# RWKV pairs pipelined: the next pair of heads' projections among the present pair's block steps, its last norm beside the next pair's levels

## The reference, cut to what matters

```python
r, k, v = jnp.einsum('ibtd,ide->ibte', xm[:3], w_rkv)
w = -jax.nn.softplus(-(w0 + jnp.tanh(xw @ w1) @ w2)) - 0.5
decay = jnp.exp(-jnp.exp(w))
a = jax.nn.sigmoid(a0 + (xa @ a1) @ a2)
g = jax.nn.sigmoid(xg @ g1) @ g2
kk = heads(k * k_k);  kk = kk / max(norm(kk), 1e-12)
kf = heads(k * (1.0 + (a - 1.0) * k_a))
def step(S, inp):                       # over the tokens, per head
    sa = einsum('bhij,bhj->bhi', S, -kk_t)
    S = S * w_t + sa (x) (kk_t * a_t) + v_t (x) k_t
    return S, einsum('bhij,bhj->bhi', S, r_t)
yn = (y - mean) * rsqrt(var + GN_EPS) * ln_w + ln_b     # per head
out = ((yn + sum(rf * kf * r_k) * vf) * g) @ w_o
```

## Time and profile before

| | us |
|---|---|
| median of 3 runs | 4031.53 |
| lowest and highest | 4029.28, 4032.35 |
| the profiled execution | 4034.49 |
| its span, first to last instruction | 4032.7 |
| busy TensorE, VectorE, ScalarE, GpSimd | 3435.5, 2789.6, 1501.1, 1424.4 |

### The profile page before, as it was taken

One profiled execution on the slowest core, in us unless ns is written; L12 is line 12 of the kernel. 1 busy time (PEld: TensorE's weight loads), 2 busy tenths in 40 slices (PEclk: granted clock), 3 DMA queues, 4 the chain that ended last, 5 costly groups with the idle time before them and its releaser, 6 DMA issues.

```text
span 4032.7 us, 46671 instructions
## 1 busy us (share of the span) xinstructions
PE 3435.5 (85%) x15384; PEld 1899.4 (47%) x15384; DVE 2789.6 (69%) x6464; ACT 1501.1 (37%) x4296; POOL 1424.4 (35%) x1272
## 2 busy tenths in 40 slices
PE   5999988869988888988989888989899888778876
PEld 3777777645443333444445443545454333333322
DVE  5555555545766666888886777898857777777775
ACT  1333333313433333534444434433435343333333
POOL 0011100013544444434443444333335444444442
PEclk8888999889999999999999999999999999999999
DMA  2110000049999999999999999999989999999996
GB/s 78 29 31 24 25 24 24 17 169 399 427 427 427 427 427 426 413 391 424 409 405 399 415 426 425 399 347 346 358 338 421 427 425 427 426 427 426 427 424 291
DMA packets 229603, 1310.45 MB, mean 325 GB/s; under 512 B 58736, under 2 KB 61936, under 8 KB 81648
## 3 DMA queue, kind: packets, MB, share of 16 engines
q0 software_dynamic: 165888, 1208.03, 72.3%
q1 hardware_dynamic: 63472, 99.43, 7.0%
HBM read 1301.52 MB, written 5.86 MB: 324 GB/s over the span
## 4 chain that ended last, share of the span: by engine, by line
DMA 30%; PE 25%; DVE 18%; ACT 3%; issue 2%; DVEq 1%; ACTq 1%; POOL 0%; POOLq 0%
DMA arena<-in_uv,arena 30%; PE psum L1157 15%; DVE arena L1585 8%; PE psum L1121 4%; PE psum L1209 3%; DVE arena L1675 3%; ACT wbuf L1375 1%; DVE arena L1649 1%; DVE arena L1513 1%; PE psum L1168 1%; ACT arena L1370 1%; PE psum L1229 1%; DVE arena L1510 0%; DVE arena L1652 0%; DVE arena L1517 0%
## 5 line engine op out<-in xcount | busy, mean ns | idle before, releaser
L1157 PE MATMUL psum<-arena,wbuf 128*128 128x512 f32 (+1 forms) x4608 | 2096.5, 629 | 442.9 <-ACT wbuf L1375 441.7
L1101 POOL DMA_INDIRECT arena<-in_uv,arena x1152 | 1349.8, 1172 | 1825.1 <-PE psum L1157 1677.9
L1585 DVE SCALAR_TENSOR_TENSOR arena<-arena 128x1024 f32<-128x1024 f32 x1152 | 1393.4, 1222 | 530.8 <-DMA arena<-in_uv,arena 514.8
L1157 PEld LDWEIGHTS psum<-arena,wbuf 128*128 128x128 f32 (+1 forms) x4608 | 811.0, 191 | 1533.2 <-issue 785.8
L1366 ACT ACTIVATE arena<-arena 128x2 f32<-128x2 f32 x576 | 116.9, 203 | 1666.9 <-DVE arena L1585 1666.1
L1375 ACT ACTIVATE wbuf<-cst,arena 128x128 f32<-128x128 f32 (+1 forms) x1152 | 392.7, 388 | 41.3 <-issue 1.7
L1121 PE MATMUL psum<-arena,wbuf 128*128 128x256 f32 (+1 forms) x1024 | 290.8, 430 | 8.7 <-DVE arena L1596 5.8
L1370 ACT ACTIVATE arena<-arena 128x1 f32<-128x1 f32 x1152 | 276.9, 287 | 40.7 <-issue 1.0
L1121 PEld LDWEIGHTS psum<-arena,wbuf 128*128 128x128 f32 x1024 | 203.3, 201 | 127.9 <-issue 88.8
L1675 DVE SCALAR_TENSOR_TENSOR arena<-arena,par 128x256 f32<-128x256 f32 x368 | 177.6, 483 | 47.8 <-ACT arena L1431 32.1
L842 POOL COPY arena<-arena 128x256 f32<-128x256 f32 x8 | 3.2, 397 | 584.0 <-DVE arena L735 584.0
(11 more groups left out here) (265 smaller groups left out, 3213.1 us busy)
## 6 DMA issues: line engine op xcount, KB each, us to landing
wbuf<-in_w_q SPq DMA_DIRECT2D x64, 576.0 KB, 9.2
arena<-in_w_pw SPq DMA_DIRECT2D x48, 512.0 KB, 10.4
arena<-in_uv,arena POOLq DMA_INDIRECT x1152, 19.0
wbuf<-in_w_rkv SPq DMA_DIRECT2D x24, 512.0 KB, 3.6
wbuf<-in_w_o SPq DMA_DIRECT2D x8, 512.0 KB, 3.5
arena<-in_w_o SPq DMA_DIRECT2D x8, 512.0 KB, 7.7
x<-in_x SPq DMA_DIRECT2D x1, 2304.0 KB, 8.1
arena<-in_state SPq DMA_DIRECT2D x16, 128.0 KB, 3.0
```

The costliest lines, as they stand in the source:

```text
L1101: pool.indirect_dma_start(ring[:, g % RING, :], None, I["uv"][p // 2], bass.IndirectOffsetOnAxis(ap=idx[:, s % 4, j:j + 1], axis=0)).then_ ...
L1157: last = pe.matmul(out, diag[:, g % DIAGS, 0:P if u < NB else NS], ring[:, g % RING, D + e * 512:D + (e + 1) * 512], start=head == 0 and j ...
L1585: stt(out=row, in0=row, scalar=1.0, in1=tok[p % 2][:, UNITS[p % 2].index(u), :], op0=ALU.mult, op1=ALU.mult, accum_out=dots[:, g % COLS:g ...
```

## The change

The passes are written out as a pipeline over pairs.

- **Projections.** A generator `front(n)` yields after each product of pair n: 2 steps for `w` with `a` (now per half of the columns, banks 2 and 3), 48 products for `k`, `r` and `v`, and 2 sums of the norm. In pass i, TensorE's block steps draw from `front(i + 1)` at fifteen places, 48 steps in all (1 ahead of R0, 1 ahead of U0, 2 ahead of Y0, 6 ahead of R1, then 3, 3, 5, 3, 3, 4, 3, 3, 3 up to Y3, 4 behind it and 4 behind `s_Y`), and the last 4 behind the mean. `front(0)` stands ahead of the first pass. All of it uses banks 2 and 3; R, U and S now share bank 0, and Y stands in bank 1. ScalarE's evictions are made per half and stand among the copies of R and U; VectorE's front stands among the state updates.
- **Last norm.** `last_norm(i - 1)` is a generator too: reciprocal in four parts, scale, bias and gain, bonus, gate. VectorE takes two steps of it after each of the first five levels of pass i.
- **Samples' state.** The two operations L821 and L823 move from before the norm to behind pass i + 1's masks, ahead of its first level.
- **Transposes.** `tok_v`, `tok_b` and `tok_k` move from ahead of the grams into levels 1, 2 and 3.
- **Buffers.** `g_s`, `bon`, `esc` and `ln` become double; `y_s`, `yc`, `ysq`, `sd`, the samples' scratch, `sc_state`, `s_tmp`, `r_tok` and `u_tok` move into `K.x`. So `x` is loaded again: six chunks behind the last samples' state, two behind the last `y`; L1605 waits for them.
- **SyncE.** Weights of pair i + 1 are asked for behind the last use of pair i's, `low2` and `prm` behind them; the samples' states are stored and loaded as before, further down the queue.

```diff
@@ wkv, buffers
-    y_s, yc, ysq, sd = e_pos, e_neg, e_prev, nrm
+    g_s = [f(), f()]
+    bon = [None, f()]
+    Q3 = Region(K.x.rearrange("p c n -> p (c n)"))
+    s_pick, s_rows = Q3.cut(SB, P), Q3.cut(P)
+    s_factors, s_vv = Q3.cut(4, NS), Q3.cut(2, NS)
+    sc_state, s_tmp = [Q3.cut(P) for _ in range(2)], Q3.cut(P)
+    r_tok, u_tok = Q3.cut(P), Q3.cut(P)
+    bon[0], y_s = Q3.cut(N), Q3.cut(N)
+    Q3 = Region(Q3.tensor, X_EARLY * N)
+    yc, ysq = Q3.cut(N), Q3.cut(N)
+    sd, s_prod = ysq, s_pick
@@ sync
+            for i in range(C):
+                if i < C - 1:
+                    for j, name in enumerate(("k1", "r1", "v1")):
+                        sp.wait_ge(pe_s.sem, pe_s.value(f"{name}.{i}"))
+                        sp.dma_start(K.w[j], I["w_rkv"][3 * (i + 1) + weight[j]]).then_inc(wl[j], 16)
...
+                sp.wait_ge(dve_s.sem, dve_s.value(f"s_state.{i}"))
+                if i == C - 1:
+                    sp.dma_start(K.x[:, 0:X_EARLY, :], I["x"][:, 0:X_EARLY, :]).then_inc(x_back, 16)
+                for e in range(2):
+                    q = of_head(e)
+                    sp.dma_start(I["o_wkv_s"][i, q], s_state[q, :, q]).then_inc(s_stored, 16)
+                if i < C - 1:
+                    sp.wait_ge(s_stored, i * 32 + 32)
+                    load_state(i + 1)
+            sp.wait_ge(dve_s.sem, dve_s.value(f"y.{C - 1}"))
+            sp.dma_start(K.x[:, X_EARLY:C, :], I["x"][:, X_EARLY:C, :]).then_inc(x_back, 16)
+            sp.wait_ge(p_stored, C * 32)
+            sp.wait_ge(s_stored, C * 32)
@@ tensor: front(n), each product followed by a yield
+                    if h:
+                        pe.wait_ge(act_s.sem, act_s.value(f"a0.{n}"))
...
+                pe.wait_ge(act_s.sem, act_s.value(f"a1.{n}"))
+                for h in range(2):
+                    yield from project(n, xm[1], 0, h, "k")
+                pe.wait_ge(wl[1], n * 16 + 16)
+                pe.wait_ge(act_s.sem, act_s.value(f"k0.{n}"))
+                yield from project(n, xm[0], 1, 0, "r")
+                pe.wait_ge(act_s.sem, act_s.value(f"k1.{n}"))
+                norm_sums(n, 1)
+                yield
+                pe.wait_ge(act_s.sem, act_s.value(f"r0.{n}"))
+                norm_sums(n, 0)
+                yield
+                pe.wait_ge(act_s.sem, act_s.value(f"n1.{n}"))
+                yield from project(n, xm[0], 1, 1, "r")
...
@@ the steps of each engine, in its order; + stands for pair i + 1, - for pair i - 1
+    pe_s = Steps(K.sem("wkv_pe"), passes("wa0 wa1 k0 k1 r0 n1 n0 r1 v0 v1",
+                 ["g", "bonus"] + [f"gram_{x}{e}" for x in ("L", "LT", "G", "RB", "RK") for e in range(2)]
+                 + [x for l in range(1, LEVELS) for x in (f"turn{l}_0", f"y{l}_0", f"turn{l}_1", f"y{l}_1",
+                                                         {1: "tok_v", 2: "tok_b", 3: "tok_k"}.get(l), f"dXT{l}_0", f"dXT{l}_1") if x]
+                 + "+wa0 R0 s_tok s_gram0 s_gram1 +wa1 U0 Y0 S0 +k0 s_y1 R1 s_d1 U1 Y1 S1 +k1".split()
+                 + "s_y2 R2 s_d2 U2 +r0 +n1 Y2 S2 +n0 s_RT R3 U3 +r1 s_U Y3 S3 +v0 s_Y mean +v1 s_S var".split()))
+    act_s = Steps(K.sem("wkv_act"), passes("w0 a0 w1 a1 k0 k1 exps r0 n1 n0 r1 v0 v1",
+                  ["g", "gram_L0", "gram_L1"]
+                  + [x for l in range(1, LEVELS) for x in (f"X{l}_0", f"y{l}_0", f"X{l}_1", f"y{l}_1",
+                                                          {1: "tok_v", 2: "tok_b", 3: "tok_k"}.get(l)) if x]
+                  + "+w0 +a0 R0 s_tok +w1 +a1 U0 +k0 s_y1 R1 U1 +k1 s_y2 R2 U2 +exps +r0 +n1 +n0".split()
+                  + "R3 U3 +r1 s_U +v0 Y +v1 ysq sd".split()))
+    dve_s = Steps(K.sem("wkv_dve"), passes("logs kf kk rk factors",
+                  ["bonus"] + [f"{x}{e}" for x in ("maskLT", "level0_") for e in range(2)]
+                  + [f"gram{x}{e}" for x in ("G", "RB", "RK") for e in range(2)] + ["-s_state"]
+                  + [f"XT{l}_{e}" for l in range(1, LEVELS - 2) for e in range(2)] + ["-y"]
+                  + [f"XT{l}_{e}" for l in range(LEVELS - 2, LEVELS) for e in range(2)]
+                  + "s_gram state0 +logs s_X1 state1 +kf s_X2 state2 s_RT state3 +kk s_y s_exp +rk yc +factors s_prod".split()))
@@ tensor, block steps
+                fill(1)
+                pe.wait_ge(act_s.sem, act_s.value(f"tok_k.{i}"))
+                pe.wait_ge(dve_s.sem, dve_s.value(f"XT{LEVELS - 1}_1.{i}"))
                 rows_R(0)
...
+                fill(1)
                 rows_U(0)
+                fill(2)
                 rows_Y_S(0)
...
+                fill(6)
+                sample_y(1)
+                rows_R(1)
+                fill(3)
+                sample_d(1)
+                rows_U(1)
+                fill(3)
+                rows_Y_S(1)
+                fill(5)
...
@@ vector
+            def last_norm(i):
+                dve.wait_ge(act_s.sem, act_s.value(f"sd.{i}"))
+                for part in range(4):
+                    reciprocal(sd, part)
+                    yield
+                dve.drain()
+                tt(yc, yc, sd, ALU.mult)
+                yield
+                dve.drain()
+                ts(yc, yc, ln[:, i % 2, 0:1], ln[:, i % 2, 1:2], ALU.mult, ALU.add)
+                yield
+                dve.drain()
+                tt(yc, yc, bon[i % 2], ALU.add)
+                yield
+                dve.drain()
+                for y, t in zip(y_out, (slice(0, T // 2), slice(T // 2, N))):
+                    last = tt(y[:, i, :], yc[:, t], g_s[i % 2][:, t], ALU.mult)
+                last.then_inc(dve_s.at(f"y.{i}"), 1)
...
+                if i:
+                    new_sample_state(i - 1)
+                    dve.wait_ge(p_stored, i * 32)
...
+                    if l < LEVELS - 1:
+                        next(behind, None)
+                        next(behind, None)
@@ retrieval_and_conv, vector
+                    if n == "wA" and c in (0, X_EARLY):
+                        dve.wait_ge(x_back, 16 if c == 0 else 32)
```

More of the change, by code:

```diff
@@ L287, in wkv @@
     G, RB, RK = (R.cut(2, NB, P) for _ in range(3))
+    g_s = [f(), f()]
+    bon = [None, f()]
+    state, s_state = R.cut(P), R.cut(SB, P)
     Q0 = Region(K.arena, dead_at)
@@ L336, in wkv @@
+    pool_s = Steps(K.sem("wkv_pool"), passes("", ["s_copies"]
+                   + [f"co{l}_{e}" for l in range(1, LEVELS - 1) for e in range(2)] + ["XT_sides"]))
     assert NB == 4 and SLEVELS == 3
@@ L613, in _ @@
+                last.then_inc(pe_s.at(f"mean.{i}"), 1)
+                for _ in ahead:
+                    pass
+                pe.wait_ge(dve_s.sem, dve_s.value(f"s_exp.{i}"))
                 for h in range(2):
@@ new lines, in _ @@
+            act.wait_ge(prm_loaded, 16)
+            for h in range(2):
+                decay_and_rate(0, h)
+            for h in range(2):
+                key(0, h)
+            for part in range(3):
+                exps(0, part)
+            receptance(0, 0)
+            key_norm(0, 1)
+            key_norm(0, 0)
+            receptance(0, 1)
+            for h in range(2):
+                value(0, h)
+            for i in range(C):
+                n, more = i + 1, i < C - 1
+                act.wait_ge(pe_s.sem, pe_s.value(f"g.{i}"))
+                act.activation(halves(g_s[i % 2]), of_banks(ps, 4), ACT.Copy).then_inc(act_s.at(f"g.{i}"), 1)
+                for e, bank in enumerate((6, 7)):
+                    act.wait_ge(pe_s.sem, pe_s.value(f"gram_L{e}.{i}"))
@@ new lines, in _ @@
+            logs(0)
+            rated_key(0)
+            norm_floor(0)
+            for part in range(4):
+                reciprocal(nrm, part)
+            unit_key(0)
+            bonus_terms(0)
+            dve.drain()
+            make_factors(0)
+            for i in range(C):
+                n, more = i + 1, i < C - 1
+                behind = last_norm(i - 1) if i else iter(())
+                dve.wait_ge(act_s.sem, act_s.value(f"v1.{i}"))
+                dve.wait_ge(pe_s.sem, pe_s.value(f"bonus.{i}"))
+                tt(halves(bon[i % 2]), of_banks(ps, 2), halves(v_s), ALU.mult).then_inc(dve_s.at(f"bonus.{i}"), 1)
@@ L837, in _ @@
+            new_sample_state(C - 1)
+            for _ in last_norm(C - 1):
+                pass
         @block.gpsimd
```

658 lines of the change are left out of this document (336 added, 322 removed).

## The result

The changed kernel takes **4013.0 us** (median of 6 runs, 3999.6 to 4017.8) where the kernel before, on the same chip, takes 4030.9. The ratio is 0.9949, with an interval of 0.993 to 0.9967. (The ratios given here are not quite the quotients of the medians.) The kernel is faster, by 18 us by the medians and by 13 to 28 by the interval, and not by 87: the forecast of 3944.5 misses, and so does its range, which ended at 3995. The profiled execution took 4014.7.

The account below looks back on a forecast made before the run. One chain through VectorE and TensorE, neither full, bounds the pass. With front and norm off it, passes take 76.5 us: seven intervals 535.5 for 626.7, gain 91.2, ends +4.3, net -87, so 3944.5 us; 8-in-10 range 3905 to 3995.

Parts of the forecast that it names:

- Grams and levels: From the grams' start to the last level's end: 25.7 us a pass, including 2.45 for the samples' state's two operations.
- Rival 2: TensorE's clock keeps falling in the block steps: 6.5 us a pass lost, 3990 us; chance 0.12.
- The pass at full clock: One pass of the RWKV stage: 75.0 us from the engine-by-engine sum, 76.5 with switching and contention added.
- two unknown costs: Per pass: switching between small and large products, 0.8 us, and contention of VectorE and GpSimd, 0.7.
- The walk: Engine by engine from level 6's delivery of `XT`: 36.5 us set by TensorE, then VectorE's 12.8; grams start at 49.3.
- Rival 1: In-order R and U copies and state updates come late in the block steps: pass 80.5, 3972 us; chance 0.13.
- Rival 4: Mixed 64-row and 128-row products before S3 hold the clock at 1.2 GHz: pass 111, 4190 us; chance 0.04.
- rival 5: The change does not overlap, as a wait ahead of the front's first piece delays everything: 4035 us; chance 0.02.
- The last norm costs nothing: Its parts fit VectorE's some 2 us idle in each level; without that cover 6.8 us a pass would come back.
- Contention: VectorE operations with two SBUF inputs lose 0.33 us beside GpSimd; 0.7 a pass added, bounds 0 and 2.
- SyncE's queue: Next weights, `low2` and `prm` wait behind the samples' states: margin 5 us, priced at nothing; each us over costs 1 per pass.
- The ends: First and last pass: pair 0's grams 2.3 later, last pass +3.4, stores behind the hidden reload +1 (0 to 3); +4.3 altogether.

Follow-up runs that it names:

- e5: e1 with SyncE asking for the next pair's weights, `prm` and `low2` ahead of its wait for the samples' state; 3948.5 us, ratio 0.9793.
- e3: Changed kernel with one of the samples' state's two operations left ahead of level 1's first addition, the other behind it; 3959.7 us, ratio 0.9831.
- e7: Changed kernel with four constant products behind level 1's last product, filling TensorE's wait, nothing moved; 3964.8 us, ratio 0.9841.
- e1: Changed kernel with the samples' state's two operations moved behind level 1's additions and the last norm one level later; 3961.7 us, ratio 0.9835.
- e6: e5 with the last samples' stores ahead of the reload of `x` and a semaphore for each part of `x`; 3944.2 us, ratio 0.9782.
- e4: Kernel before the change, with two VectorE products of unused scratch ahead of level 1's additions; 4116.4 us, ratio 1.0211.
- e8: e4 with four constant products on TensorE behind level 1's last product, filling the wait; 4043.0 us, ratio 1.003 to the kernel before.
- e2: Changed kernel with five constant products on TensorE ahead of level 1's last product, nothing moved; 3970.8 us, ratio 0.9852.
- e9: e6 with a one-column Sigmoid on ScalarE behind level 6, so the activation table loads early; 3937.3 us, ratio 0.9776.

## Why the prediction was wrong

**What failed** is the step "Grams and levels", in the sentence that prices the two operations of the samples' state at 2.45 us because "they delay the chain fully". As a delay it is nearly right: 12.6 us less the 9.6 of before is 3.0 with the transposes moved away, and against e5's 10.7 it is 1.9. But it was priced as time alone. The wait it opens on TensorE (1.81 us) brings the levels behind it to a clock of 0.50 to 0.75, which costs 4.2 to 10.9 us a pass. For the seven intervals that is 40.2 us (the levels' excess over 15.5), and 3.9 more in each of two block stretches: 48 of the 58 us by which the intervals exceed my 535.5 less the 2.45 of pass 0. At full clock the changed pass is 12.6 + 15.5 + 49.4 = 77.5, 1.0 over the forecast's, and pass 0, which I had taken to be shorter by the state it lacks (74.05), takes 77.9: together the remaining 10 us. The last pass, 91.3 us from L858 to the barrier where e5 takes 77.0, carries 10.9 more.

**Rival 2**, "the clock keeps falling", had the right mechanism, at the wrong place and price: I looked for it in the block steps, where the clock had been low, with half of 13 us, 6.5 a pass, and there no fall began before the last pass, whose steps have no front to fill them. It came in the levels, which had been at 1.00 in every pass of before (one of them in the earlier trace rows). Its bound of 3990 carried the range's end, so the range missed too. Where a product's stretch runs at full clock, a change that puts a wait of such a length ahead of it has to be priced at half the clock for that stretch: 11 us here, 76 in seven passes, which would have put the forecast at about 4021.

The kernel before had such a wait, and I passed it over. Late in the block steps of every pass TensorE waits 1.94 us for L806, and in all eight passes the clock is at 0.50 no later than 1.2 us behind the wait's end; the earlier trace rows has the 10 us that follow this one:

```profile
435.61 0.41 PE L598 MATMUL psum<-arena 64*64 64x64 f32 x4 [1.94 <-DVE arena L806]
```

What the Trainium skill ("TensorE: Matmul & The Clock Gate", "What's actually happening") says, that activity releases the throttle, holds for the block steps as I used it: filled with the next pair's products they run at 1.00. The levels disagree with a plain reading of it. TensorE's row is busy for 26.08 of 26.4 us there, and the clock stays at 0.50 to the end.

Point by point, the other steps:

- **The pass at full clock**: forecast 75.0 + 1.5 for the two unknown costs; the changed kernel's is 77.5. That e5 has 76.4 is luck in part, since there the state's operations, 2.45 in the sum, no longer delay the chain. The walk was 1.8 us short from the last copy's end to L: it has 36.5 + 12.8 = 49.3, and e5 takes 51.1 (lines below: that copy, the state's update behind S3, `s_prod`, the last product ahead of the grams, and L). S3 came at 38.3 and not at 36.5. From there VectorE took 12.5, as forecast (12.8), but TensorE took 12.9 where I had "about 11", because the sum left out the products of `g` and of the bonus (L476 and L481), 1.0 us each, which stand ahead of the grams. So TensorE and not VectorE decided when L began. The two unknown costs (0.8 for switching, 0.7 for contention) were not separated; the 1.8 us by which S3 was late hold the first, with whatever else the walk had too short.

```profile
295.65 0.74 DVE L934 COPY arena<-psum 64x256 f32<-64x256 f32 x2
334.66 0.35 DVE L941 SCALAR_TENSOR_TENSOR x<-psum,arena,cst 128x128 f32<-128x128 f32 x1 [1.30 <-PE psum L580]
345.90 1.22 DVE L1009 TENSOR_TENSOR x<-psum,cst 128x512 f32<-128x512 f32 x2
346.42 1.13 PE L481 MATMUL psum<-arena,cst 128*128 128x288 f32 x4
347.49 1.63 PE L454 MATMUL psum<-arena 64*64 64x64 f32 x80
```

- **Rival 1** (late copies) did not come: at full clock no pass is longer than 77.9.
- **Rival 4** (mixed products at 1.2 GHz) is refuted by the 1.00 of the mixed stretch, and rival 5 by the passes of 76.4.
- **The last norm costs nothing** beside the levels: they take 15.5 us in pass 0, without it, and as much in three of e3's passes, with it and one of the state's operations.
- **Contention**: L862 takes 1.61 us beside GpSimd's work and L864, in the gap behind it, 1.23, so it lost 0.38 where I had 0.33. The Trainium skill ("SBUF — State Buffer", "Who interferes with whom") has the two engines lock each other out for a whole instruction; the row stays within that, at about half of one of GpSimd's products of 0.7 us, and far from the 8 us that the lock would have cost at its worst.
- **SyncE's queue**: the margin held in the changed kernel, and in e7 as well, whose levels ran at full clock: behind the first pair's, TensorE waits for `low2` in neither. In e1 it was gone: the operations came later by a level, the issues and the landing took longer (6.1 us from issue to use for `low2`, where I had 3.6), and the price was not 1 us for each us but again the clock's. The three passes with that wait took 12 us more than e5's; the rest of the 14.6 between the two (551.0 and 536.4) is mostly the stops in the levels.
- **The ends**: L858 of pair 0 came at 113.5, 2.0 earlier than before and not 2.3 later. The barrier stands 2.0 us behind the last `y` where it stood 0.3 behind before, so the stores behind `x` cost 1.7, within 0 to 3; in e6 it stands at 0.9. The reload itself is hidden, as said.

e1 takes the loss away by moving two operations, e7 takes it away without moving any, and e4 and e8 make and unmake it in the kernel before. That settles the mechanism, not what in the chip sets the length of a fall.

## What to carry to other kernels

When work is moved onto VectorE's path between two of TensorE's small products, price the wait it opens twice: once as time, once as the following stretch of products at half clock, and look for the stretches that run at 1.00 now, because only those can lose it. Put such work behind the operation on which TensorE waits, or, where that can't be, let TensorE make constant products into an unused bank; in e8 four of them per pass, 2.2 us, gave back 73. And re-read each queue's margin whenever an operation moves on which that queue waits: in e1 a move by one level made `low2` late, and its wait costs the clock as well.

## What the hardware showed that was not expected

- A wait of 1.8 us (2.5 in e4) between 64-row products is followed by 0.50 with TensorE busy nearly all along, for 10.2, 13.7 or 37.6 us in the changed kernel, and for 51.2 in its last pass. The first line below is one whole fall of 37.6. Equal passes fell into kinds for that reason: 81.8 and 83.4 us with the short falls, 92.3 with the long ones. What sets the length was not settled.
- How long a wait has to be can't be said from these runs by its length alone. Where passes are mixed, all seven waits and stops of 1.37 to 1.88 us in e1, e2 and e3 have a fall at them or within 2.4 us behind, and so has e7's of 0.94. Four stops of 0.85 to 0.89 have none. The wait of 0.76 has one in 2 of 18 passes (both in e6, none in e5 and e9), and none of the waits of 0.49 to 0.56 has.
- A wait of 1.6 us stands ahead of the grams in the kernel before, and the clock keeps 1.00 there in all eight passes (12.7 us in sum). The second and third line below are that wait in one pass and the levels of a pass. Why that one never brings the clock down and level 1's does was not settled. The two differ in what runs ahead: there 128-row products of the front, here the grams' and level 1's 64-row products. That can't be all, as the 1.94 us of before, which always do, stand behind 128-row products too, though with gaps between them.
- TensorE seems to have run out of instructions while the weights were loaded: all 15 stops of 0.4 to 1.9 us in the levels of e1, e2, e3 and e7 end 1.3 to 1.6 us behind a piece of the program's instructions.

```profile
287.41:324.96 37.55, 37.20 (x494) 33.19 (x494) 13.05 (x40) 11.77 (x30) 3.78 (x6) 0.50 0.21 62
```

```profile
389.97 1.09 PE L439 MATMUL psum<-cst,arena 128*128 128x128 f32 x8 [1.59 <-DVE arena L735]
```

```profile
307.80:322.00 14.20, 14.20 (x442) 14.05 (x443) 2.92 (x11) 6.54 (x20) 4.47 (x7) 1.00 0.02 5
```
